# Loading the pieces of the first eight modulation parts two raw chunks sooner on SyncE's queue

## The chip, the cores and the metric

The kernel runs on one core of a Trainium2 chip. The metric is the device time of one execution in microseconds (us), and smaller is better. Three runs of the kernel before gave 2529.38 us in the median (2528.78 to 2529.84). One further execution was recorded by the hardware profiler.

The engines are named as in the profile: PE multiplies matrices, DVE does elementwise work on vectors, ACT applies activations and copies, POOL does little here, and SP only issues transfers (DMAs). Each engine runs its own list of instructions in order, and engines wait for one another through semaphores. All transfers that matter here are issued by SP and go through one queue, which 16 DMA engines serve.

## The reference

Two transformer-like blocks are computed for one sequence of 256 tokens with 2048 features, in float32. The first block begins so:

```python
c_act = jax.nn.silu(c)
mod = c_act @ w_ada[l] + b_ada[l]                 # [2048] x [2048, 12288]
sh1, sc1, gt1, sh2, sc2, gt2 = jnp.split(mod, 6)
h = modulate(rmsnorm(x, g_norm_mix[l]), sh1, sc1)  # h * (1 + sc1) + sh1
proj = h @ w_in[l]                                 # [256, 2048] x [2048, 3072]
```

After it come a recurrent mixer and a pooling mixer, an output product, and a gated feed-forward product; the second block (attention and retention) has no modulation. Only the stretch that the lines above describe is touched by the change. The product with `w_ada` is a vector times a matrix of 100 MB, so it is mostly a matter of bringing the matrix in. The product with `w_in` is real work for PE, but needs `h`, and `h` needs the first two sixths of `mod`, the shift `sh1` and the scale `sc1`.

## The kernel before

**Raw chunks.** Every weight matrix of the big products comes in as chunks of 512 KB (`raw`, 128 partitions x 1024 values). There are 8 buffers for raw chunks. ACT rounds a chunk to its high part (line 1020), DVE subtracts to get the low part (line 1390), and both parts lie in one of 4 buffers (`split`). PE multiplies high and low parts separately (lines 650 and 657 in the wide form, lines 630 to 632 in the narrow form). A chunk is numbered G; PE works through the chunks in order. At step G of their loops, ACT and DVE first finish the sum of chunk G (ACT copies the low half of it from PSUM in the wide form, line 1027; DVE adds it up and so clears the PSUM bank, lines 1410 and 1398) and then convert chunk G + 4. PSUM has two banks for these sums, so PE may begin chunk G once DVE has evacuated chunk G - 2.

**The first product, by quarters.** The 2048 rows of `w_in` are cut into four units of 512. Chunks 0 to 11 hold unit 0 for the 12 column slabs, chunks 12 to 23 unit 1, and chunks 24 to 47 units 2 and 3. So PE can begin with unit 0 of `h` as soon as unit 0 of the modulation is there.

**Pieces and rides.** The columns of `w_ada` for scale and shift of the four units are eight narrow parts (n = 0 to 7: scale and shift of unit 0, then of unit 1, and so on). Each narrow part is loaded in 4 pieces of 1024 KB (`ride`), so there are 32 narrow pieces. They share 4 slots; a piece may be loaded once PE has multiplied the piece four before it (semaphore `ada_multiplied`, line 487 stands behind that wait). The first 8 pieces are multiplied before chunk 0. The other 24 ride in pairs: the list `RIDE_AT` says behind which chunk PE multiplies a pair (line 675): behind chunks 2, 4, 6, 8, 9, 11, 13, 15, 16, 18, 20 and 21. Below, pieces have the numbers 0 to 31, and "the pair of chunk 9" is the one that rides behind chunk 9 (pieces 16 and 17).

**What DVE does with them.** When the four pieces of a part are multiplied, DVE turns the row to columns. For a scale part (`scale_unit`, lines 1441, 1443, 1572, 1529) it also scales the four blocks of `x`; for a shift part (`shift_unit`, lines 1441, 1443, 1534) it makes the low part of `h` after ACT made the high part (line 1074). These steps stand in DVE's loop over G behind the conversion of chunk G + 4: scale of units 1, 2 and 3 at steps 5, 12 and 19, shift of units 1, 2 and 3 at steps 9, 16 and 22. At step 14 stands a short chain on constants of the recurrence (lines 1586 to 1603).

**SP's order.** SP's queue is one list in program order. `LOAD_AT` says before which raw chunk each riding piece is loaded:

```python
        for G in range(2, DOWN_0 + CHUNKS * OUT_SLABS):
            for r, at in enumerate(LOAD_AT):
                if at == G:
                    ...
                        sp.wait_ge(ada_multiplied, free)
                    load_ada(slot, *piece_of(piece))
            ...
            load(G // (2 * CHUNKS), G % (2 * CHUNKS), src)
```

`load` (line 476) waits until the chunk 8 before has been converted. Since SP works in order, a raw chunk that stands behind a pair of pieces is issued only after the waits of that pair.

Pieces after the 31st are wide and belong to later parts (loaded before chunks 30, 36, 38 and so on); still later rows of `w_ada` are added up by DVE.

Of the kernel before, what the change touches and what calls it, by code (L numbers as in the profile page):

```python
# [86 lines left out]
FIRST_WIDE = NARROW * NARROW_PIECES  # L87
# [31 lines left out]
FIRST_RIDE = EARLY * NARROW_PIECES  # L119


def _rides():

    at = [at for at in (2, 4, 6, 8, 9, 11, 13, 15, 16, 18, 20, 21) for _ in range(2)]
    return at + [at for at, _, _ in LATE]


RIDE_AT = _rides()
LOAD_AT = [at + 4 for at in RIDE_AT[:FIRST_WIDE - FIRST_RIDE]]
LOAD_AT += [load for _, _, load in LATE]  # L130
assert len(LATE) == TENSOR_PIECES - FIRST_WIDE
LAST_RIDE = {n: RIDE_AT[min(last_piece(n) - FIRST_RIDE, len(RIDE_AT) - 1)] for n in range(EARLY, TENSOR_PARTS + 1)}
# [51 lines left out]
def build(nc, dram, out):  # L184
# [284 lines left out]
    def _(sp):  # L469
# [26 lines left out]
# [3 lines that stand above are left out]
# [1760 lines left out]
```

## Time and profile before

| | |
|---|---|
| median of 3 runs | 2529.38 us (2528.78 to 2529.84) |
| the profiled execution | 2529.0 us, of which the span of the trace is 2527.1 us |
| PE busy | 2491.0 us (99%) |
| DVE busy | 1834.6 us (73%) |
| ACT busy | 1190.1 us (47%) |
| DMA, all queues | 554.69 MB, 219 GB/s over the span, 391 to 410 GB/s in its first two fortieths |

Busy time is the time in which an engine executes something; the span runs from the first to the last instruction of the trace. The 1.9 us between the span and the time of the profiled execution lie around the trace. In the timelines a row has its start in us from the start of the span, its duration in us, the engine, the line of the kernel, the operation with what it writes and reads, and in square brackets the time that the engine was idle before it with what ended that idle time. Rows of several like instructions are merged, with their count behind an x.

### The profile page before, as it was taken

To read this page: it belongs to the slowest core of one execution; us is meant where nothing else is said; L and a number is where in the kernel's file an instruction comes from. 1 tells how busy PE (TensorE), PEld (TensorE's weight loads), DVE (VectorE), ACT (ScalarE), POOL (GpSimd) and SP (SyncE) were. 2 spreads that over 40 slices of the span, in tenths; PEclk is the share of its full clock that TensorE was granted. 3 is DMA by queue.
4 is the path that set the end of the run, shared out by engine and by line. 5 is a ranking of instruction groups with operands and counts; after the bars stand their busy time and mean duration, and the time that the engine had idled before them with its cause. 6 is when DMAs were issued, how large, how long until landed. Compare 5 with 4: busy or idle time off the path is not lost.

```text
span 2527.1 us, 42169 instructions
## 1 busy us (share of the span) xinstructions
PE 2491.0 (99%) x15708; PEld 2168.1 (86%) x15708; DVE 1834.6 (73%) x2381; ACT 1190.1 (47%) x1458; POOL 18.6 (1%) x54
## 2 busy tenths in 40 slices
PE   7999999999999999999999999999999999999998
PEld 6888888888888888888888888888888888888887
DVE  5678988996556655787785665676888668875886
ACT  3365445544444444654454554455544444444444
POOL 0000000000000000000000000000000000000000
PEclk9999999999999999999999999999999999999999
DMA  9999978797666665566555556556555655566554
GB/s 391 410 391 370 361 265 273 245 342 229 186 189 189 191 202 170 179 204 196 181 165 172 166 184 191 184 192 191 175 199 184 191 187 178 190 200 183 185 173 125
DMA packets 165238, 554.69 MB, mean 219 GB/s; under 512 B 16624, under 2 KB 20720, under 8 KB 165120
## 3 DMA queue, kind: packets, MB, share of 16 engines
q1 hardware_dynamic: 163728, 549.85, 65.0%
q0 software_dynamic: 1392, 3.22, 0.4%
q8 instruction: 80, 1.31, 0.2%
q14 instruction: 38, 0.31, 0.0%
HBM read 550.38 MB, written 2.10 MB: 219 GB/s over the span
## 4 chain that ended last, share of the span: by engine, by line
PE 89%; DVE 6%; DMA 2%; issue 2%; ACT 1%; SPq 0%; DVEq 0%; ACTq 0%
PE ps L650 52%; PE ps L657 26%; PE ps L647 2%; DMA ride<-in_w_ada 2%; PE pm L675 2%; DVE split L1390 2%; DVE acc_ada L1456 1%; PE ps L630 1%; PE ps L654 1%; PE ps L631 1%; PE ps L632 1%; ACT split L1020 0%; DVE val L1408 0%; PE pm L806 0%; DVE x_t L1556 0%
## 5 line engine op out<-in xcount | busy, mean ns | idle before, releaser
L1390 DVE TENSOR_TENSOR split<-raw,split 128x1024 fp32r<-128x1024 f32 (+1 forms) x864 | 1030.8, 1204 | 583.3 <-ACT split L1020 578.6
L1020 ACT ACTIVATE split<-raw 128x1024 fp32r<-128x1024 f32 (+1 forms) x864 | 895.7, 1042 | 1054.3 <-PE ps L657 938.1
L650 PE MATMUL ps<-h_s,split 128*128 128x512 f32 x3592 | 1134.4, 397 | 4.5 <-DVE h_s L1534 2.5
L657 PEld LDWEIGHTS ps<-h_s,split 128*128 128x128 f32 x3592 | 675.9, 188 | 159.9
L650 PE MATMUL ps<-mid_s,split 128*128 128x512 f32 x2336 | 735.0, 396 | 1.0 <-DVE split L1390 0.8
L657 PE MATMUL ps<-h_s,split 128*128 128x256 f32 x3592 | 706.7, 278 | 0.0
L650 PEld LDWEIGHTS ps<-h_s,split 128*128 128x128 f32 x3592 | 548.6, 189 | 9.3 <-issue 5.6
L657 PEld LDWEIGHTS ps<-mid_s,split 128*128 128x128 f32 x2336 | 438.8, 188 | 103.8
L657 PE MATMUL ps<-mid_s,split 128*128 128x256 f32 x2336 | 458.9, 278 | 0.0
L650 PEld LDWEIGHTS ps<-mid_s,split 128*128 128x128 f32 x2336 | 355.6, 189 | 5.0 <-issue 2.7
L1027 ACT ACTIVATE low<-ps 128x512 f32<-128x512 f32 x238 | 138.2, 581 | 22.4 <-PE ps L657 22.4
L1864 DVE SCALAR_TENSOR_TENSOR conv_o<-up_pad,par,conv_o 128x256 f32<-128x256 f32 x176 | 77.5, 482 | 11.4 <-DVE conv_o L1862 5.6
L630 PE MATMUL ps<-h_s,split 128*128 128x256 f32 x288 | 83.6, 290 | 0.0
L631 PE MATMUL ps<-h_s,split 128*128 128x256 f32 x288 | 81.4, 283 | 0.0
L632 PE MATMUL ps<-h_s,split 128*128 128x256 f32 x288 | 81.4, 283 | 0.0
L647 PE MATMUL ps<-split,h_s 128*128 128x512 f32 x256 | 80.8, 397 | 0.0
L675 PE MATMUL pm<-ride,c_act 128*1 128x128 f32 (+1 forms) x1248 | 47.9, 302 | 18.2 <-DMA ride<-in_w_ada 18.2
L1456 DVE SCALAR_TENSOR_TENSOR acc_ada<-add_ffn,c_act,acc_ada 128x1024 f32<-128x1024 f32 x51 | 65.2, 1279 | 0.0
L1410 DVE TENSOR_TENSOR val<-ps,low 128x512 f32<-128x512 f32 x92 | 62.9, 684 | 2.6 <-ACT low L1027 2.6
L1412 DVE TENSOR_TENSOR low<-ps,low 128x512 f32<-128x512 f32 x88 | 60.2, 685 | 3.8 <-ACT low L1027 3.6
L630 PEld LDWEIGHTS ps<-h_s,split 128*128 128x128 f32 x288 | 55.1, 191 | 4.8 <-issue 4.4
L654 PEld LDWEIGHTS ps<-split,h_s 128*128 128x128 f32 x256 | 48.1, 188 | 11.4
(285 smaller groups left out, 1485.4 us busy)
## 6 DMA issues: line engine op xcount, KB each, us to landing
raw<-in_w_in SPq DMA_DIRECT2D x224, 512.0 KB, 3.6
raw<-in_w_ffn_down SPq DMA_DIRECT2D x128, 512.0 KB, 4.2
ride<-in_w_ada SPq DMA_DIRECT2D x46, 1024.0 KB, 11.7
raw<-in_w_ffn_gate SPq DMA_DIRECT2D x88, 512.0 KB, 3.8
raw<-in_w_ffn_up SPq DMA_DIRECT2D x88, 512.0 KB, 4.2
raw<-in_w_ffn_a SPq DMA_DIRECT2D x88, 512.0 KB, 4.1
raw<-in_w_ffn_b SPq DMA_DIRECT2D x88, 512.0 KB, 4.4
raw<-in_w_out SPq DMA_DIRECT2D x64, 512.0 KB, 4.3
```

Of the source, the lines that this page charges most:

```text
L630: pe.matmul(ps[:, s, b, 0:T], weights[:, 0, :], x[:, 0, :], start=start, stop=False)
L631: pe.matmul(ps[:, s, b, 0:T], weights[:, 0, :], x[:, 1, :], start=False, stop=False)
L632: mm = pe.matmul(ps[:, s, b, 0:T], weights[:, 1, :], x[:, 0, :], start=False, stop=stop)
L647: pe.matmul(ps[:, s, b, :], acts[:, k0 + k, 0, b * P:(b + 1) * P], split[:, slot, k, :, :].rearrange("p h n -> p (h n)"), start=start, sto ...
L650: pe.matmul(ps[:, s, b, :], split[:, slot, k, 0, b * P:(b + 1) * P], acts[:, k0 + k, :, :].rearrange("p h t -> p (h t)"), start=start, sto ...
L657: mm = pe.matmul(ps[:, s, b, 0:T], split[:, slot, k, 1, b * P:(b + 1) * P], acts[:, k0 + k, 0, :], start=False, stop=stop)
L675: mm = pe.matmul(pm[2 + n % 2][32 * g:32 * g + 1, 0:32 * blocks].rearrange("p (j q) -> p j q", j=blocks), weights, wide[:, g, :, :], start ...
L1020: act.activation(split[:, c, 0:kt, 0, :], raw[:, CHUNKS * s + c, 0:kt, :], ACT.Copy).then_inc(hi_ready, 1)
L1027: act.activation(low[:, s, :, :], ps[:, s, :, T:2 * T], ACT.Copy).then_inc(low_copied, 1)
L1390: dve.tensor_tensor(split[:, c, 0:kt, 1, :], raw[:, CHUNKS * s + c, 0:kt, :], split[:, c, 0:kt, 0, :].bitcast(F32), ALU.subtract).then_inc ...
L1456: dve.scalar_tensor_tensor(out=sums, in0=piece, scalar=c_act[:, k:k + 1], in1=sums, op0=ALU.mult, op1=ALU.add).then_inc(ada_added, 1)
L1864: ins = dve.scalar_tensor_tensor(out=dst, in0=src, scalar=w, in1=dst, op0=ALU.mult, op1=ALU.add)
```

## The change

The number added to a ride's chunk in `LOAD_AT` falls from 4 to 2 for the 24 narrow riding pieces (8 to 31):

```diff
-LOAD_AT = [at + 4 for at in RIDE_AT[:FIRST_WIDE - FIRST_RIDE]]
+LOAD_AT = [at + 2 for at in RIDE_AT[:FIRST_WIDE - FIRST_RIDE]]
 LOAD_AT += [load for _, _, load in LATE]
```

So the twelve pairs are loaded before raw chunks 4, 6, 8, 10, 11, 13, 15, 17, 18, 20, 22 and 23, where before they stood ahead of chunks 6, 8, 10, 12, 13, 15, 17, 19, 20, 22, 24 and 25. The wide pieces stay where they are. The lists of PE, DVE, ACT and POOL are the same in both kernels; only SP's list differs.

The first place is the start of SP's list, from raw chunk 0 on. `ride` and `ride_89` are two halves of the four slots, and a row stands for like transfers in a row. Before:

```order
L476 DMA raw<-in_w_in 128x1024
L487 DMA ride_89<-in_w_ada 128x4x512 x2
L476 DMA raw<-in_w_in 128x1024 x5
L487 DMA ride<-in_w_ada 128x4x512 x2
L476 DMA raw<-in_w_in 128x1024 x2
L487 DMA ride_89<-in_w_ada 128x4x512 x2
L476 DMA raw<-in_w_in 128x1024 x2
```

And now, at the same place:

```order
L476 DMA raw<-in_w_in 128x1024
L487 DMA ride_89<-in_w_ada 128x4x512 x2
L476 DMA raw<-in_w_in 128x1024 x3
L487 DMA ride<-in_w_ada 128x4x512 x2
L476 DMA raw<-in_w_in 128x1024 x2
L487 DMA ride_89<-in_w_ada 128x4x512 x2
L476 DMA raw<-in_w_in 128x1024 x2
```

The first raw row is chunk 0, and the first pair is pieces 6 and 7. Between pieces 7 and 8 the list had raw chunks 1 to 5, and has chunks 1 to 3 now. Chunks 4 and 5 have moved behind the pair of chunk 2. From there on the pattern of rows repeats with chunk numbers that are two lower: each pair stands two chunks sooner, and each chunk that it passes stands one pair later. Chunks 11 and 18 (and 23 at the end) are passed by two pairs, because the pairs of chunks 8 and 9, of 15 and 16, and of 20 and 21 ride close together.

The second place is the end of the moved stretch on SP, from the pair of chunk 18 to the first wide pair (128x2x1024). Before:

```order
L487 DMA ride_89<-in_w_ada 128x4x512 x2
L476 DMA raw<-in_w_in 128x1024 x2
L487 DMA ride<-in_w_ada 128x4x512 x2
L476 DMA raw<-in_w_in 128x1024
L487 DMA ride_89<-in_w_ada 128x4x512 x2
L476 DMA raw<-in_w_in 128x1024 x5
L487 DMA ride<-in_w_ada 128x2x1024 x2
```

And now:

```order
L487 DMA ride_89<-in_w_ada 128x4x512 x2
L476 DMA raw<-in_w_in 128x1024 x2
L487 DMA ride<-in_w_ada 128x4x512 x2
L476 DMA raw<-in_w_in 128x1024
L487 DMA ride_89<-in_w_ada 128x4x512 x2
L476 DMA raw<-in_w_in 128x1024 x7
L487 DMA ride<-in_w_ada 128x2x1024 x2
```

Behind the last narrow pair (the pair of chunk 21) now follow chunks 23 to 29, where before followed chunks 25 to 29. Chunk 23 stood ahead of the pairs of chunks 20 and 21 and now stands behind both.

## Rows read from the trace of the kernel before

**Rows 1.** The page: PE's busy time over the span, and SP's DMA queue.

```profile
PE 2491.0 (99%) x15708; PEld 2168.1 (86%) x15708; DVE 1834.6 (73%) x2381; ACT 1190.1 (47%) x1458; POOL 18.6 (1%) x54
...
q1 hardware_dynamic: 163728, 549.85, 65.0%
```

**Rows 2.** Stretches in us: length, busy PE, PEld, DVE, ACT, POOL, clock, DMA share, GB/s.

```profile
35.00:140.00 105.00, 101.04 (x1313) 90.56 (x1314) 67.63 (x115) 45.13 (x60) 4.47 (x7) 1.00 1.04 405
44.00:52.00 8.00, 8.00 (x115) 6.84 (x117) 3.91 (x5) 3.54 (x5) 0.00 (x0) 1.00 1.04 411
...
180.00:200.00 20.00, 20.00 (x204) 16.77 (x206) 14.76 (x23) 15.76 (x27) 0.00 (x0) 1.00 0.85 336
```

**Rows 3.** PE's waits from 33 to 140 us: total, times, longest.

```profile
PE pm L675 <- DMA ride<-in_w_ada: 3.6, 3, 2.3
PE ps L650 <- DVE h_s L1534: 0.8, 1, 0.8
```

**Rows 4.** PE's waits from 140 us to the end, the longest in total.

```profile
PE pm L760 <- DVE diag L1503: 2.1, 2, 1.1
PE ps L650 <- DVE h_s L1534: 1.7, 1, 1.7
```

**Rows 5.** PE's timeline: starts of chunks 8, 12, 17, 19, 22; two late rides.

```profile
63.93 0.63 PE L650 MATMUL ps<-h_s,split 128*128 128x512 f32 x2
...
81.66 0.39 PE L630 MATMUL ps<-h_s,split 128*128 128x256 f32 x1
...
103.66 1.05 PE L675 MATMUL pm<-ride,c_act 128*1 128x128 f32 x32 [2.28 <-DMA ride<-in_w_ada]
104.65 0.39 PE L630 MATMUL ps<-h_s,split 128*128 128x256 f32 x1
...
112.44 0.39 PE L630 MATMUL ps<-h_s,split 128*128 128x256 f32 x1
...
125.37 1.05 PE L675 MATMUL pm<-ride,c_act 128*1 128x128 f32 x32 [1.00 <-DMA ride<-in_w_ada]
126.36 0.39 PE L630 MATMUL ps<-h_s,split 128*128 128x256 f32 x1
```

**Rows 6.** ACT's timeline: conversions of chunks 8, 13, 17, 18, 19, 20, 23.

```profile
52.67 1.06 ACT L1020 ACTIVATE split<-raw 128x1024 fp32r<-128x1024 f32 x1 [0.41 <-DMA raw<-in_w_in]
...
74.28 1.06 ACT L1020 ACTIVATE split<-raw 128x1024 fp32r<-128x1024 f32 x1 [1.92 <-DMA raw<-in_w_in]
...
89.53 1.06 ACT L1020 ACTIVATE split<-raw 128x1024 fp32r<-128x1024 f32 x1 [3.58 <-DMA raw<-in_w_in]
92.69 1.06 ACT L1020 ACTIVATE split<-raw 128x1024 fp32r<-128x1024 f32 x1 [2.10 <-PE ps L632]
...
97.21 1.06 ACT L1020 ACTIVATE split<-raw 128x1024 fp32r<-128x1024 f32 x1 [1.81 <-DMA raw<-in_w_in]
104.87 1.06 ACT L1020 ACTIVATE split<-raw 128x1024 fp32r<-128x1024 f32 x1 [6.60 <-DMA raw<-in_w_in]
...
115.69 1.06 ACT L1020 ACTIVATE split<-raw 128x1024 fp32r<-128x1024 f32 x1 [1.95 <-PE ps L632]
```

**Rows 7.** DVE's timeline: conversion of chunk 9; evacuations of chunks 6, 10, 15, 17, 20.

```profile
58.15 1.23 DVE L1390 TENSOR_TENSOR split<-raw,split 128x1024 fp32r<-128x1024 f32 x1 [0.33 <-ACT split L1020]
...
61.62 0.69 DVE L1410 TENSOR_TENSOR pool_x<-ps,low 128x512 f32<-128x512 f32 x1
...
79.35 0.69 DVE L1410 TENSOR_TENSOR gate_p<-ps,low 128x512 f32<-128x512 f32 x1
...
98.78 0.69 DVE L1398 TENSOR_TENSOR xr_pad<-ps,xr_pad 128x512 f32<-128x512 f32 x1
...
109.94 0.68 DVE L1398 TENSOR_TENSOR pool_x<-ps,pool_x 128x512 f32<-128x512 f32 x1
...
120.31 0.69 DVE L1398 TENSOR_TENSOR val<-ps,val 128x512 f32<-128x512 f32 x1
```

**Rows 8.** SP's timeline: issue of the pairs of chunks 16 and 21.

```profile
88.71 1.81 SPq L487 DMA_DIRECT2D ride<-in_w_ada  x2
...
111.70 2.26 SPq L487 DMA_DIRECT2D ride<-in_w_ada  x2
```

**Rows 9.** Pieces by line 487, issue to landing: first 300 us, then first 130 us.

```profile
DMA to landing us min/median/max: 4.8/11.7/18.9
...
DMA to landing us min/median/max: 7.9/12.5/18.9
```

## The prediction

> **What bounds the kernel now.** I read the page first: PE is busy for 2491.0 us of the span, 99%, and SP's queue takes 65.0% of the DMA engines' time over the whole run [rows 1]. So PE bounds the kernel as a whole, and a change of SP's order can matter only where PE waits. Next came the stretches. From 35 to 140 us PE is busy for 101.04 of 105 us, while the DMA share is 1.04 at 405 GB/s; from 180 us on the share falls to 0.85 [rows 2]. So in the stretch that the change touches the queue is full all the time, and PE nearly so. Then PE's waits: from 33 to 140 us it waits 3 times for a piece, 3.6 us in all, the longest 2.3 us [rows 3]. Afterwards it waits for no transfer; its largest groups are 2.1 and 1.7 us on DVE [rows 4]. So what PE has lost or won when chunk 22 begins stays until the end, and I work out just that: PE's start of chunk 22, 126.36 us before [rows 5].
>
> **What the queue does.** With the queue full, the moment at which a transfer lands depends on the bytes ahead of it alone. At 411 GB/s [rows 2] a pair of pieces (2 x 1.049 MB) takes 5.10 us and a raw chunk (0.524 MB) 1.28 us. Two raw chunks and a pair make 7.66 us. The trace has the same period: chunk 19 ends ACT's wait at 97.21 and chunk 20, one pair and one chunk later, at 104.87 [rows 6]; this is 7.66 where 6.38 is due, so 1.28 us of it is a single lateness, which I keep as a separate term. The change deletes and adds no transfer. It lets each pair land sooner by the one or two raw chunks that it passes, 1.28 to 2.56 us, and each passed chunk later by 5.10 us, or 10.2 us for chunks 11, 18 and 23.
>
> The Trainium skill (SBUF — State Buffer, Summary: rules for kernel authors) says to reckon about 358 GB/s for the time of transfers between HBM and SBUF. By that a pair would take 5.86 us and each chunk would be 0.76 us later than I say. The trace moved 411 GB/s [rows 2], so the measurement decides.
>
> **What is removed.** The three late rides, 3.6 us [rows 3]; 2.28 and 1.00 us of them are the second pieces of the pairs of chunks 16 and 21 [rows 5]. Their pieces land 2.5 us and 2.6 us sooner, so I count all of it as gone.
>
> **What is late next: the raw chunks.** They look well covered, since ACT and DVE convert four chunks ahead. But the cover is shorter than it looks. PE may begin chunk G when DVE has evacuated chunk G - 2, and in DVE's list that evacuation stands behind the conversion of chunk G + 1. So chunk G + 1 must have landed, been converted by ACT and DVE, and chunk G - 2 evacuated, before PE begins G. Where a scale or shift step stands between the two, that is added. I take each path from its own rows and shift its landing.
>
> - Chunk 8. Raw chunk 8 landed at 52.67 [rows 6] and now at 57.77. Then ACT 1.06, DVE 1.23, an evacuation 0.69, and from the conversion of chunk 9 (with the scale step of unit 1) to the end of the evacuation of chunk 6 62.31 - 58.15 = 4.16 us [rows 7]. The sum is 64.9 to 65.0 us, where PE began at 63.93 [rows 5]: +1.0.
> - Chunk 12. Raw chunk 13 landed at 74.28 and the evacuation of chunk 10 ended at 79.35 + 0.69 = 80.04, with the shift step of unit 1 between: 5.76 us [rows 6, 7]. Now 74.28 + 5.10 + 5.76 = 85.14, where PE began at 81.66 [rows 5]: +3.5.
> - Chunk 17. PE carries +3.5 into it and wins back the wait of 2.28 us: +1.2 without a new wait. Raw chunk 18 now stands behind the pair of chunk 16, whose second piece landed at 103.62 (0.04 before its ride [rows 5]); without chunk 19 ahead it is 102.3 us, or 101.1 if the single lateness of 1.28 us falls behind it. ACT began this chunk at 92.69 and the evacuation of chunk 15 ended at 99.47, with the chain of constants between: 6.78 us [rows 6, 7]. So PE begins at 109.2 (or 107.9) against 104.65 [rows 5]: +4.5 (or +3.3).
> - Chunk 19. At PE's own pace the same shift. Raw chunk 20: 104.87 + 5.10 + (110.62 - 104.87) = 115.7 against 112.44 [rows 5 to 7]: +3.3, not above what PE carries.
> - Chunk 22. PE wins back 1.00 us: +3.5 (or +2.3). Raw chunk 23 now lands where the last piece landed, less chunk 24: 125.33 - 1.28 = 124.05. From ACT's start at 115.69 to the end of the evacuation of chunk 20 at 121.00 it took 5.31 us [rows 6, 7]. So PE begins at 129.4 at the soonest, against 126.36 [rows 5]: +3.0.
>
> **Does the queue run dry?** Every pair waits until the pair two before it has been multiplied, and now more of SP's list stands behind that wait. The pair of chunk 16 was issued at 88.71 [rows 8] on the ride behind chunk 13, which is 3.5 us later now: 92.2. To follow raw chunk 17 (89.53 + 5.10 = 94.6 [rows 6]) without a gap, its first piece must land at 97.2, 5.0 us after issue. The pair of chunk 21 was issued at 111.70 [rows 8] on the ride behind chunk 18: with +4.5 this is 116.2, and it should land at 120.2, 4.0 us after issue. What a piece takes that meets an empty queue no row shows just so. From below, the shortest landing in the first 300 us is 4.8 us; from above, the shortest in the loaded stretch is 7.9 us [rows 9]. I take 4.8, since the 7.9 us of the loaded stretch are mostly waiting behind other bytes. By 4.8 the first has no gap and the second one of 0.8 us, which puts chunk 22 at 130.2: +3.9. With +3.3 at chunk 17 there is no gap, and chunk 22 stands at +3.0. Between these I take +3.5.
>
> The Trainium skill (DMA: Bandwidth & Descriptors, Anatomy of one DMA) gives about 2.0 us plus bytes over 436 GB/s for a DMA on the GpSimd path, which would be an estimate of 4.4 us for a piece; the gap would be 0.4 us, and the end +3.5. No run here shows a lone piece that fast, so the bound from the row stays.
>
> Nothing else changes: the other engines' lists are the same, and the pieces' slots are given free by the same rides. Chunk 25 and all behind it have the same bytes ahead of them as before, and PE comes to them 3 us later, so they have more cover than before.
>
> **The sum.** Old waits go, -3.6; new waits come, +7.1 (1.0 at chunk 8, 2.8 at chunk 12, 2.1 to 3.3 at chunk 17, what is left by chunk 22), so that chunk 22 begins 3.5 us later. The profiled execution took 2529.0 us (span 2527.1 and 1.9 around it), 0.4 under the median of the runs. The forecast is 2529.4 + 3.5 = 2532.9 us, +0.14%. A change below 0.2%, some 5.1 us, is about what a measurement of this kernel cannot tell from none, so I call this the same, on the slow side.
>
> **Rivals.**
> A. The raw chunks have enough cover, and only the late rides go. For it: ACT's conversions start four chunks ahead, and two of those I use began on PE's signal with the chunk long landed (92.69 and 115.69 [rows 6]). Against it: five of the seven rows there end on the DMA. The time would be 2529.4 - 3.6 = 2525.8 us.
> B. The loop of rides, slots and loads feeds on itself, so that the kernel is slower by more than the bound. Its place is SP's wait for a slot: once a pair is issued later than the queue needs it, every chunk behind is late by the gap, PE rides later still, and the next pair is issued later. It decides from the point at which a pair meets an empty queue. With 7.9 us a piece in place of 4.8, the pair of chunk 16 leaves a gap of 2.9 us, and that of chunk 21 at least 1.6 us more: 3.5 + 4.5 = +8.0, 2537.4 us. For it: margins of 0.2 and -0.8 us above. Against it: the queue's backlog in that stretch is why 7.9 was seen.
> C. The order changes little, because the pairs are issued on the rides anyway, at the same instants. Then the pieces land hardly sooner, and the chunks find the queue emptier than I reckon: within 1 us of before, 2529.4 us. Against it: the queue is full at 1.04 [rows 2], so each byte that is moved ahead delays what is behind it.
>
> **How the numbers follow.** The forecast (+1.5 to +5) has 0.61, A (-3.6 to -1) 0.12, B (above +5.1) 0.19, C 0.08. A can pass -0.2% only if PE gained more than the 3.6 us that it waits, so faster gets 0.02; slower is B and a little of the forecast's edge, 0.20; the same has the rest, 0.78. The range leaves out most of A below and the upper part of B above: 2528.5 to 2536.5 us.
>
> **What would show it.** Right: PE's wait for pieces after 33 us falls to almost nothing, and PE waits for evacuations by DVE instead, at chunk 8 (about 1 us), chunk 12 (2.8), chunk 17 (2 to 3) and, smaller, near chunk 22; ACT waits longer for raw chunks; PE begins chunk 12 near 85.1 and chunk 22 near 129.9; behind it PE has no new wait. Wrong: if PE begins chunk 12 before 83, raw chunks are not 5.10 us later, or the path from landing to PE is shorter; if the DMA share falls below 1 between 90 and 125 us by more than a slice, the queue ran dry and B holds; if the shift at chunk 22 does not stay until the end, something behind absorbs it.

## The result and the profile after

The changed kernel takes 2537.24 us in the median of 7 runs (2534.98 to 2539.99), the kernel before 2529.21 us (2527.98 to 2529.84) beside it. The ratio is 1.0034, with a 95% interval of 1.0025 to 1.0043: slower by some 8.0 us. The forecast was 2532.9 us with a range up to 2536.5, so the time lies outside. One of the twelve executions of the kernel e5 below took 4947.2 us and counts in neither its median nor its ratio.

The page of the changed kernel, in the two lines that answer to [rows 1]:

```profile
PE 2491.9 (98%) x15708; PEld 2170.5 (86%) x15708; DVE 1833.2 (72%) x2381; ACT 1190.2 (47%) x1458; POOL 18.6 (1%) x54
...
q1 hardware_dynamic: 163728, 549.85, 64.7%
```

Over the span PE is busy for 0.9 us more than before and idle for 7.4 us more. That does not say that it loses by waiting alone, since a chunk at a lower clock counts as busy. Its waits from 33 to 145 us, as in [rows 3]:

```profile
PE ps L630 <- DVE xr_pad L1398: 3.3, 1, 3.3
PE ps L630 <- DVE gate_p L1410: 2.7, 1, 2.7
PE ps L630 <- DVE val L1398: 2.0, 1, 2.0
PE ps L650 <- DVE pool_x L1410: 1.0, 1, 1.0
```

The waits for pieces are gone, 3.6 us of them, and four waits for evacuations by DVE stand in their place, 9.0 us. PE's timeline shows where they are; these are the starts of chunks 8, 12, 17, 18, 19, 22 and 23, where [rows 5] had the starts around them:

```profile
65.05 0.50 PE L650 MATMUL ps<-h_s,split 128*128 128x512 f32 x1 [0.96 <-DVE pool_x L1410]
...
85.31 0.39 PE L630 MATMUL ps<-h_s,split 128*128 128x256 f32 x1 [2.68 <-DVE gate_p L1410]
...
109.23 0.58 PE L630 MATMUL ps<-h_s,split 128*128 128x256 f32 x1 [3.31 <-DVE xr_pad L1398]
...
114.52 0.41 PE L630 MATMUL ps<-h_s,split 128*128 128x256 f32 x1
...
119.46 0.39 PE L630 MATMUL ps<-h_s,split 128*128 128x256 f32 x1
...
134.23 0.39 PE L630 MATMUL ps<-h_s,split 128*128 128x256 f32 x1 [1.96 <-DVE val L1398]
...
138.68 0.29 PE L630 MATMUL ps<-h_s,split 128*128 128x256 f32 x1
```

Chunks 8, 12 and 17 begin at 65.05, 85.31 and 109.23, where the forecast had 65.0, 85.1 and 109.2. Up to here it holds to 0.2 us. Then it fails: the row at 114.52 is the start of chunk 18, so chunk 17 took 5.29 us, against 2.97 from chunk 17 to 18 in the trace of before. The row at 138.68 is the start of chunk 23; chunk 22 took 4.45 us. The stretches tell why. Columns as in [rows 2], the clock and the DMA share at the end of a row:

```profile
93.00:101.00 8.00, 8.00 (x121) 7.45 (x113) 3.13 (x5) 1.06 (x1) 0.00 (x0) 1.00 0.99 346
109.20:114.50 5.30, 5.27 (x24) 5.27 (x25) 3.44 (x5) 1.47 (x2) 0.00 (x0) 0.50 1.04 412
115.00:119.00 4.00, 4.00 (x75) 3.80 (x77) 3.82 (x7) 1.75 (x3) 0.00 (x0) 1.00 0.67 263
134.00:138.70 4.70, 4.47 (x25) 4.48 (x26) 3.22 (x4) 0.00 (x0) 1.53 (x3) 0.64 1.04 343
```

During chunk 17 the granted clock of TensorE is 0.50, that is 1.2 of 2.4 GHz, right behind PE's wait of 3.31 us; during chunk 22 it is 0.64 in the mean, behind a wait of 1.96 us. (The clock falls in the wait itself: from 106.0 to 109.0 us, while PE does nothing, it is 0.83.) And the DMA share, 1.04 before from 35 to 140 us [rows 2], falls to 0.99 and 0.67 in two stretches, and the rate from 405 to 346 and 263 GB/s: the queue ran short. SP's issues of the pairs of chunks 16 and 21, as in [rows 8]:

```profile
92.38 1.88 SPq L487 DMA_DIRECT2D ride<-in_w_ada  x2
...
118.72 1.24 SPq L487 DMA_DIRECT2D ride<-in_w_ada  x2
```

The first pieces of the two took 5.9 and 5.0 us to land (the view of DMA issues, in windows that hold one piece each; the last column is the time from issue to landing):

```profile
ride<-in_w_ada SPq DMA_DIRECT2D x1, 1024.0 KB, 5.9
...
ride<-in_w_ada SPq DMA_DIRECT2D x1, 1024.0 KB, 5.0
```

ACT's conversions of chunks 17, 18, 20, 22 and 23, as in [rows 6], all end on the DMA now:

```profile
94.75 1.06 ACT L1020 ACTIVATE split<-raw 128x1024 fp32r<-128x1024 f32 x1 [5.13 <-DMA raw<-in_w_in]
102.42 1.06 ACT L1020 ACTIVATE split<-raw 128x1024 fp32r<-128x1024 f32 x1 [6.60 <-DMA raw<-in_w_in]
...
111.25 1.06 ACT L1020 ACTIVATE split<-raw 128x1024 fp32r<-128x1024 f32 x1 [5.18 <-DMA raw<-in_w_in]
...
119.33 1.06 ACT L1020 ACTIVATE split<-raw 128x1024 fp32r<-128x1024 f32 x1 [2.58 <-DMA raw<-in_w_in]
128.86 1.06 ACT L1020 ACTIVATE split<-raw 128x1024 fp32r<-128x1024 f32 x1 [8.47 <-DMA raw<-in_w_in]
```

The first piece of the pair of chunk 16 could have landed at 94.7 + 2.55 = 97.3, right behind raw chunk 17; it landed at 92.38 + 5.9 = 98.3, so the gap is 1.0 us. That of the pair of chunk 21 could have landed at 119.3 + 2.55 = 121.9 and came at 118.72 + 5.0 = 123.7: a gap of 1.8 us. The raw chunks behind came later still. A pair and a chunk take 6.38 us in a full queue; from chunk 17 to 18 it took 102.42 - 94.75 = 7.67 us, and from chunk 22 to 23 128.86 - 119.33 = 9.53 us, so chunk 18 lost 1.3 us and chunk 23 3.15 us. Why chunk 23 lost more than the gap ahead of its pair is not shown. After chunk 23 PE has no new wait above 0.2 us.

The starts of PE's chunks in the kernels that follow, as differences in us to the trace of before (one profiled execution each; chunk 0 itself varies by up to 0.6 us):

| kernel | 8 | 12 | 17 | 18 | 19 | 22 | 23 |
|---|---|---|---|---|---|---|---|
| changed kernel | +1.1 | +3.65 | +4.6 | +6.9 | +7.0 | +7.9 | +9.35 |
| e1, idle products at 12, 17, 22 | +1.4 | +3.9 | +4.95 | +4.95 | +5.4 | +5.8 | +5.7 |
| e2, idle products at 17 | +1.7 | +4.2 | +6.5 | +6.5 | +6.5 | +7.2 | +8.7 |
| e3, first six pairs sooner | +1.3 | +3.7 | +1.3 | +1.3 | +1.3 | +0.1 | +0.1 |
| e4, last six pairs sooner | +0.1 | +0.1 | +3.35 | +4.9 | +4.9 | +5.8 | +5.8 |
| e6, constants first | +1.3 | +3.7 | +1.25 | +1.3 | +4.8 | +5.3 | +5.3 |
| e7, three chunks behind | +0.5 | +0.1 | -0.9 | -0.7 | -0.6 | -1.2 | -0.9 |
| e8, three pairs alone | +0.2 | +0.2 | -1.2 | -0.9 | +0.05 | -1.0 | -0.7 |

e5 has two pairs of rides elsewhere, so of it the chunks with the same work ahead are told below.

### The profile page after: what moved, and what is told of

Its sections match the earlier page's. It is cut to its first block, busy times and chain, and to the rows that moved or that the text cites. A ratio compares the mean times of both kernels' runs of the same rounds, so it can differ in the third digit from the quotient of the medians.

```text
span 2535.4 us, 42169 instructions
## 1 busy us (share of the span) xinstructions
PE 2491.9 (98%) x15708; PEld 2170.5 (86%) x15708; DVE 1833.2 (72%) x2381; ACT 1190.2 (47%) x1458; POOL 18.6 (1%) x54
## 4 chain that ended last, share of the span: by engine, by line
PE 87%; DVE 7%; DMA 3%; issue 2%; ACT 1%; SPq 0%; DVEq 0%; ACTq 0%
PE ps L650 52%; PE ps L657 25%; PE ps L647 2%; DMA raw<-in_w_in 2%; DVE split L1390 2%; DVE acc_ada L1456 1%; PE ps L630 1%; PE ps L631 1%; PE ps L632 1%; PE ps L654 1%; PE pm L675 1%; DMA ride<-in_w_ada 1%; ACT split L1020 1%; DVE val L1408 0%; PE pm L806 0%
```

## The experiments

The theory after the result: the late bytes do what the forecast says; what came on top is that PE's clock falls to half at a wait, and that the queue has gaps where SP waits for a slot. The rival is B of the prediction: the loop of rides, slots and loads grows by itself.

**e1 and e2: PE kept busy.** Products that nothing reads are multiplied ahead of PE's waits, in the changed kernel; e2 has `{17: 12}` alone.

```diff
         def quarter_slab(G):
+            keep_busy({12: 8, 17: 12, 22: 7}.get(G, 0))
             if G >= 2:
                 pe.wait_ge(evacuated, G - 1)
```

Expected of e1:

> The changed kernel, with idle products (128x128, nothing reads them) on PE ahead of its waits at chunks 12 (8 of them, 2.0 us), 17 (12, 3.0 us) and 22 (7, 1.8 us), so that PE works through the waits. Theory (PE's clock falls to half after a wait, and the products at half clock are what came on top of the waits): the granted clock stays 1.00 from 109 to 139 us, chunk 17 takes 2.97 us where it took 5.3, chunk 22 begins 4 to 5 us later than before and not 7.9, and the time is 2533 to 2534 us, near what was forecast. Rival (the loop of rides, slots and loads feeds on itself, the clock does not matter): 2536.5 to 2538, as the changed kernel.

Measured: 2534.22 us, ratio 1.0022 (1.0012 to 1.0031). The same stretches of e1:

```profile
109.20:114.50 5.30, 4.90 (x41) 4.90 (x42) 3.50 (x5) 1.06 (x1) 0.00 (x0) 1.00 1.03 406
115.00:119.00 4.00, 3.65 (x80) 3.15 (x79) 3.48 (x7) 2.51 (x5) 0.00 (x0) 1.00 0.94 332
134.00:138.70 4.70, 4.70 (x42) 4.70 (x41) 3.41 (x5) 1.58 (x3) 0.00 (x0) 1.00 1.04 301
```

The clock is 1.00 in all three, chunk 17 takes 2.97 us again, and the DMA share from 115 to 119 us is 0.94 where it was 0.67. The loss against the kernel before (2528.79 us beside it) is 5.4 us where it was 8.0, so holding the clock up is worth 2.6 us of the median; but the time is above the expected 2534 by 0.2 us, and chunk 22 begins 5.8 us late where 4 to 5 was expected. Something besides the clock was still missing. ACT's conversions of chunks 17, 18, 22 and 23 in e1:

```profile
95.01 1.06 ACT L1021 ACTIVATE split<-raw 128x1024 fp32r<-128x1024 f32 x1 [5.14 <-DMA raw<-in_w_in]
102.77 1.06 ACT L1021 ACTIVATE split<-raw 128x1024 fp32r<-128x1024 f32 x1 [6.71 <-DMA raw<-in_w_in]
...
119.53 1.06 ACT L1021 ACTIVATE split<-raw 128x1024 fp32r<-128x1024 f32 x1 [2.02 <-DMA raw<-in_w_in]
126.66 1.06 ACT L1021 ACTIVATE split<-raw 128x1024 fp32r<-128x1024 f32 x1 [6.07 <-DMA raw<-in_w_in]
```

From chunk 17 to 18 it is 7.76 us and from chunk 22 to 23 7.13 us, so 1.4 and 0.75 us are still lost in the queue at full clock; the second gap has shrunk with the slow chunk.

Expected of e2:

> The changed kernel, with 12 idle products ahead of the wait at chunk 17 alone. Theory (clock): chunk 17 takes 2.97 us, so 2.3 us go there, and the gap in the queue at the pair of chunk 21 shrinks by up to 1.8 us; the wait at chunk 22 may still bring the clock down (1.5 us). 2533.5 to 2535.5 us. Rival (loop): 2536.5 to 2538.

Measured: 2535.69 us, ratio 1.0029 (1.0019 to 1.0038), a little above the range of the theory and below that of the rival. In its profile chunk 17 has its full clock, but half clock came behind the wait at chunk 12 instead. PE's row at that chunk, and the stretches of chunks 12 and 22:

```profile
85.84 0.39 PE L630 MATMUL ps<-h_s,split 128*128 128x256 f32 x1 [2.68 <-DVE gate_p L1411]
```

```profile
85.80:90.30 4.50, 4.46 (x24) 4.46 (x25) 3.05 (x3) 1.75 (x3) 0.00 (x0) 0.62 1.03 406
...
133.50:138.00 4.50, 4.43 (x24) 4.43 (x25) 3.07 (x4) 0.00 (x0) 1.49 (x3) 0.62 1.04 352
```

The wait at chunk 12 is 2.68 us in this execution and in that of the changed kernel. There the clock stayed at 1.00 and chunk 12 took 2.98 us; here it took 4.5. In the profiles of e3 and e6 waits of 2.69 and 2.68 us at this chunk left the clock at full again. So the length of a wait alone does not decide.

**e3 and e4: half of the pairs.** The edit of e3; in e4 the 2 and the 4 change places.

```diff
-LOAD_AT = [at + 2 for at in RIDE_AT[:FIRST_WIDE - FIRST_RIDE]]
+LOAD_AT = [at + (2 if at <= 11 else 4) for at in RIDE_AT[:FIRST_WIDE - FIRST_RIDE]]
```

Expected of e3:

> Only the six pairs of chunks 2 to 11 are loaded two chunks sooner, those of chunks 13 to 21 stand as before. Theory (each place is one path from a landing to PE, and a later place with cover takes the shift back): chunk 8 +1.1, chunk 12 +3.65 as in the changed kernel, but chunk 17 only +1.2 to +1.5 and chunk 22 +0.2 to +0.6; 2529.4 to 2530.0 us. Rival (loop: a late ride makes the next load late, so a shift stays or grows): +3.7 or more at chunk 22, 2533 and above.

Measured: 2529.05 us, ratio 1.0001 (0.9992 to 1.0010), 0.35 us below the expected range, with chunk 22 at +0.1 where +0.2 to +0.6 was expected. PE's starts of chunks 12, 17 and 22:

```profile
85.38 0.39 PE L630 MATMUL ps<-h_s,split 128*128 128x256 f32 x1 [2.69 <-DVE gate_p L1410]
...
105.91 0.39 PE L630 MATMUL ps<-h_s,split 128*128 128x256 f32 x1
...
126.44 0.39 PE L630 MATMUL ps<-h_s,split 128*128 128x256 f32 x1
```

The wait at chunk 12 is the same as in the changed kernel, and by chunk 22 all of it has been given back, since the late rides of before (2.28 and 1.00 us [rows 5]) simply become shorter waits. So a shift of 3.7 us does not feed on itself as such. B's own place, a pair that meets an empty queue, e3 does not reach: the later pairs stand as before, and the queue stays full.

Expected of e4:

> Only the six pairs of chunks 13 to 21 are loaded two chunks sooner, those of chunks 2 to 11 stand as before. Theory (the paths of chunks 17 and 22 and the clock set the end): nothing until chunk 12, +4.6 at chunk 17 with a wait of over 4 us, chunk 17 at half clock (+2.3), a gap in the queue at the pair of chunk 21; 2535.5 to 2538 us, like the changed kernel. Rival (the shifts of the first half add to those of the second): about half of the loss, 2533.

Measured: 2535.26 us, ratio 1.0026 (1.0016 to 1.0036), 0.2 us below the expected range and far from the rival's 2533. PE waits 3.69 us at chunk 17 and 2.08 us at chunk 22; the stretch of chunk 17 and one behind it:

```profile
108.00:112.50 4.50, 4.50 (x25) 4.50 (x26) 3.01 (x4) 1.06 (x1) 0.00 (x0) 0.62 1.03 406
114.50:118.00 3.50, 3.50 (x78) 3.07 (x77) 3.21 (x5) 1.37 (x3) 0.00 (x0) 1.00 0.43 135
```

Half clock and a gap again, without any shift from the first half. Chunk 17 itself begins 1.25 us sooner than expected, and PE also waits 1.06 us at chunk 15, which was not expected. Most of the loss, 6.5 of 8.0 us, belongs to the last six pairs.

**e5: the gaps taken away.** As e1 (8, 8 and 4 idle products), and the rides of two pairs stand one chunk sooner on PE, so that SP issues the pairs of chunks 16 and 21 2.8 and 4.1 us sooner than in e1. The order of the transfers, and the step of the scale part on DVE, stay.

```diff
+RIDE_AT = [{13: 12, 18: 17}.get(at, at) if r < FIRST_WIDE - FIRST_RIDE else at for r, at in enumerate(RIDE_AT)]
...
+LAST_RIDE[6] = 18
```

> As the kernel with idle products at chunks 12, 17 and 22 (8, 8 and 4 of them here), and the rides of the pairs of chunks 13 and 18 stand one chunk sooner on PE (behind chunks 12 and 17), so that the slots of the pairs of chunks 16 and 21 come free 3 us sooner; the order of the transfers and DVE's steps stay. Theory (beside the clock, the rest over the forecast is gaps in the queue at these two pairs, where SP waits for a slot): the pair of chunk 16 lands right behind raw chunk 17 and the pair of chunk 21 right behind raw chunk 22, chunk 17 begins +3.7 to +4.5 after before and chunk 22 +3.5 to +4.5, where the kernel with idle products alone has +4.95 and +5.76; 2532 to 2533.2 us against its 2534.2. Rival (the rest is late bytes from elsewhere, the gaps are hidden): as that kernel, +5.7 at chunk 22 and 2534 to 2534.5.

Measured: 2532.11 us, ratio 1.0012 (1.0003 to 1.0021). Three stretches, PE's starts of chunks 17 and 22, and ACT's conversions of chunks 17, 18, 22 and 23 (lines are two or three higher in this kernel):

```profile
93.00:101.00 8.00, 8.00 (x114) 7.79 (x117) 3.49 (x6) 1.06 (x1) 0.00 (x0) 1.00 1.03 406
...
100.00:104.00 4.00, 4.00 (x74) 3.73 (x63) 1.30 (x2) 2.35 (x3) 0.00 (x0) 1.00 0.88 296
...
115.00:119.00 4.00, 4.00 (x35) 4.00 (x34) 2.92 (x5) 1.15 (x2) 0.00 (x0) 1.00 1.04 412
```

```profile
108.33 0.39 PE L632 MATMUL ps<-h_s,split 128*128 128x256 f32 x1
...
130.46 0.39 PE L632 MATMUL ps<-h_s,split 128*128 128x256 f32 x1 [0.43 <-DVE val L1401]
```

```profile
95.11 1.06 ACT L1023 ACTIVATE split<-raw 128x1024 fp32r<-128x1024 f32 x1 [5.17 <-DMA raw<-in_w_in]
101.50 1.06 ACT L1023 ACTIVATE split<-raw 128x1024 fp32r<-128x1024 f32 x1 [5.33 <-DMA raw<-in_w_in]
...
118.69 1.06 ACT L1023 ACTIVATE split<-raw 128x1024 fp32r<-128x1024 f32 x1 [2.85 <-DMA raw<-in_w_in]
125.09 1.06 ACT L1023 ACTIVATE split<-raw 128x1024 fp32r<-128x1024 f32 x1 [5.33 <-DMA raw<-in_w_in]
```

The two gaps are gone: from chunk 17 to 18 it is 6.39 us and from chunk 22 to 23 6.40 us, where 6.38 is due. Chunk 17 begins +3.7 and chunk 22 +4.1 after before, as expected, and the loss is 3.1 us (2532.11 against 2528.97), 2.3 us less than that of e1. The fewer idle products are not the reason: in e1 PE still waits 0.7 and 0.6 us behind them at chunks 12 and 17, and chunk 22 begins at 132.12, right behind the evacuation of chunk 20, which ends at 131.99. But the 3.1 us are not the price of the late bytes alone. From 100 to 104 us the queue runs short here too, at the pair of chunk 18, whose first piece takes 6.0 us to land; the changed kernel and e1 have the same dip (350 and 364 GB/s in that stretch), and no run takes it away. The working of the prediction had +3.0 for chunk 22 without a gap.

**e6: another path shortened.** In the changed kernel the chain of constants at step 14 moves ahead of the conversion of chunk 18, on ACT and DVE.

```diff
-            ahead(G)
             if G == LAMBDA_AT:
                 lru_constants()
+            ahead(G)
```

> The changed kernel, with the chain of constants at step 14 ahead of the conversion of chunk 18 on ACT and DVE, where DVE only waits for that chunk. Theory (each place is a path from a landing to PE): chunk 17 loses its wait of 3.3 us and begins near +1.3, but the next path, raw chunk 20 through the shift step of unit 2, is as late as before, so the wait appears at chunk 19 (about 3 us, +4.5); the gap at the pair of chunk 21 shrinks, since the ride behind chunk 18 is sooner; 2533 to 2535.5 us. Rival (the chain of constants is what the change costs): 2529.5 to 2531 us.

Measured: 2534.62 us, ratio 1.0022 (1.0013 to 1.0031). PE's start of chunk 19, and the stretch of that chunk:

```profile
117.25 0.39 PE L630 MATMUL ps<-h_s,split 128*128 128x256 f32 x1 [3.47 <-DVE pool_x L1398]
```

```profile
117.20:121.70 4.50, 4.45 (x24) 4.46 (x25) 2.45 (x3) 1.06 (x1) 0.00 (x0) 0.62 1.04 408
```

The wait at chunk 17 is gone, and the next path gives one of 3.47 us at chunk 19, with low clock behind it. The loss is 5.65 us, 2.4 us less than that of the changed kernel and far from the rival's 0.5 to 2: taking out one path helps little while the chunks of the next are as late. In this profile the pair of chunk 21 is issued at 112.96 and leaves no gap.

**e7 and e8: less of the change.** In e7 the number added to a ride's chunk in `LOAD_AT` is 3 for all pairs; in e8 it is 3 for those of chunks 9, 16 and 21 alone and 4, as before, for the others. The line of e7, and that of e8:

```diff
+LOAD_AT = [at + 3 for at in RIDE_AT[:FIRST_WIDE - FIRST_RIDE]]
...
+LOAD_AT = [at + (3 if at in (9, 16, 21) else 4) for at in RIDE_AT[:FIRST_WIDE - FIRST_RIDE]]
```

> The pairs are loaded three chunks behind their ride's number, halfway between the two kernels: each pair passes one raw chunk and each passed chunk is 5.1 us later. Theory (paths): waits of about 0.4 us at chunk 8 and 0.8 to 1.3 us at chunk 15 (raw chunk 16 through the scale step of unit 2), the late ride at chunk 16 shrinks from 2.3 to about 1 us and the others vanish; chunk 22 begins -0.5 to -1.3, 2527.5 to 2528.5 us. Rival (any passed chunk costs PE its lateness, or the loop runs): half of the loss or more, 2533.

> Only the pairs of chunks 9, 16 and 21, the ones that ride close behind another pair and came late, are loaded one raw chunk sooner. Theory: their waits shrink by 1.28 us each (to 0, 1.0 and 0), and chunks 12, 19 and 24, 5.1 us later, have cover, save perhaps chunk 24: chunk 22 begins -2 to -2.6, chunk 23 -0.9 or sooner; 2527.5 to 2528.3 us. Rival: no change that can be measured in either direction, 2528.8.

Measured: e7 2527.92 us, ratio 0.9997 (0.9988 to 1.0005), and e8 2528.15 us, ratio 0.9996 (0.9988 to 1.0005). Neither can be told from no change, though both medians are lower. In the profile of e7 PE waits 0.3 us at chunk 8 and 1.22 us at chunk 15, and begins chunk 22 1.2 us sooner than before:

```profile
93.88 0.39 PE L630 MATMUL ps<-h_s,split 128*128 128x256 f32 x1 [1.22 <-DVE xr_pad L1398]
...
125.13 0.39 PE L630 MATMUL ps<-h_s,split 128*128 128x256 f32 x1
```

Both waits are of the expected size; the late rides wait 0.4 us where about 1 was expected. In e8 chunk 22 begins 1.0 us sooner where 2 to 2.6 was expected; the late rides still wait 1.9 us in all, where 1.0 was expected. No kernel here beats the one before beyond its interval.

## Why the prediction was wrong

**Where the time went.** By medians, each against the kernel before beside it: 3.1 us are left in e5 (the late bytes, and the dip at the pair of chunk 18), 2.3 us are the gaps at the pairs of chunks 16 and 21 (e1 over e5), 2.6 us the clock with what it adds to the second gap (changed kernel over e1); together the 8.0 us measured. The split between neighbours is rougher than these digits: the intervals of e1 and e5, and of e1 and the changed kernel, overlap, and what tells the three apart are the clock, the DMA share and ACT's rows. In the profile the +9.35 us at chunk 23 are 5.4 us more of waits and 3.8 us of two slow chunks.

- *What bounds the kernel, and that the start of chunk 22 is what stays.* Right in kind: e1's +5.7 at chunk 23 stands at +5.4 in the time. But the stretch to follow ended one chunk later, since chunk 22 itself ran slow. And some 1 us did not stay: DVE's sum at 320.38 us before comes 9.34 us later in the changed kernel, that at 346.90 us 8.30 us later. Between them every profile here has a stretch of low clock; the mean clock from 320 to 360 us is 0.87 before and 0.91 in the changed kernel.
- *What is removed.* Right: no ride waits for a piece behind 33 us.
- *What is late next.* Right, path by path: chunks 8, 12 and 17 to 0.2 us; e3, e5 and e6 each moved as these paths say. At chunk 17 the size is in part luck: the forecast had raw chunk 18 at 102.3 by the lateness of 1.28 us and without a gap. It came at 102.42, but by a gap; in e5, without the gap, it came at 101.50, near the other figure of the prediction, 101.1, with the lateness behind it.
- *Does the queue run dry?* The term was mis-sized. It was priced at 4.8 us for a lone piece, which gave no gap at the pair of chunk 16 and 0.8 us at that of chunk 21. Measured were 5.9 and 5.0 us, with 2.4 and 0.6 us of other bytes still to land ahead of them, and gaps of 1.0 and 1.8 us (1.3 and 3.15 us for the raw chunks behind). The second grew because the ride behind chunk 18 came later: the pair was issued at 118.72, not 116.2. The pair of chunk 18 was not reckoned at all: it was issued at 100.18, its first piece took 7.2 us, and the queue dipped there too.
- *"Nothing else changes."* This is the step that failed. The new waits were counted as waiting only. Behind two of them PE multiplied at half clock: chunk 17 took 2.3 us and chunk 22 1.5 us more. The sum had no term for it, and neither had the range: its upper end would have had to hold the +3.9 of the forecast and some 4 us for the clock. The trace of before shows both cases. Its wait of 2.28 us at 103.66 [rows 5] was followed by a chunk of 2.97 us. But at the waits of [rows 4], which the prediction passed over, the clock did fall:

```profile
330.00:335.00 5.00, 2.60 (x8) 2.14 (x9) 3.53 (x11) 2.77 (x6) 0.00 (x0) 0.50 0.13 54
...
333.62 1.19 PE L650 MATMUL ps<-h_s,split 128*128 128x512 f32 x2 [1.72 <-DVE h_s L1534]
```

Two such matmuls take 0.63 us at 63.93 [rows 5] and 1.19 us here, behind several waits of at most 1.72 us. The Trainium skill (TensorE: Matmul & The Clock Gate, Part 1) has the 1.2 GHz as the clock of an idle TensorE; the granted 0.50 of the changed kernel agrees with that level. I had not weighed it.
- *Rival B.* Its number, 2537.4 us, was met, but by its mechanism only in part, so the agreement is luck. Its gaps were to be 2.9 and 1.6 us; they were 1.0 and 1.8. A late ride does make a late issue and a gap, as B says, at full clock too (e1 over e5, 2.3 us). What B does not have is the clock: a slow chunk makes the next ride later still, and the second gap grows from 0.75 us in e1 to 3.15 us in the changed kernel, both for raw chunk 23.
- *Rivals A and C.* Both fell: the raw chunks had too little cover, and each came later by what was moved ahead of it.

## What to carry to other kernels

When a queue is full, moving a transfer ahead makes everything that it passes later by its bytes, and a buffer of many chunks does not show how much cover there is: follow one chunk from its landing through every in-order step that stands before the engine's next start. A wait that a change puts into a dense row of matmuls costs more than its length when the clock falls at it (1.5 to 2.3 us more here), so give every new wait of PE of the size of those above a second price in the range, the next chunk at half clock, and look in the trace of before for stretches where the clock already falls. And where a queue's issue waits for a slot, compare the time from that release to the moment when the queue empties with what a transfer takes that meets a short queue (5.0 to 7.2 us here), not with the shortest one seen.

## What the runs showed of the hardware that was not expected

- TensorE at a granted clock of 0.50 behind a wait of 3.31 us, for the whole of a chunk (109.2 to 114.5 us), in a kernel that is busy 98% of its span. In the mean of some 4.5 us it was 0.62 to 0.64 behind waits of 1.86 (e2, chunk 22), 1.96 (the changed kernel, chunk 22), 2.68 (e2, chunk 12), 3.47 (e6) and 3.69 us (e4), and 1.00 behind waits of 2.08 (e4, chunk 22), 2.28 (the kernel before) and again 2.68 us (the changed kernel, chunk 12). In the kernel before it is 0.50 from 330 to 335 us, where no wait is longer than 1.72 us but PE is busy for 2.60 of 5 us. What decides between them stays open here.
- One and the same stretch of low clock differs by execution. From 320 to 360 us the mean clock is 0.87 in six of the ten profiles (before, e1, e5, e6, e7, e8) and 0.91 in four (the changed kernel, e2, e3, e4); in these four the shift against before falls by 1.0 to 1.2 us between 320 and 347 us, in the others by at most 0.3 us.
- The changed kernel spreads over 5.0 us in 7 runs, the kernel before over 1.9 us in its 7. That the clock makes this spread is only argued.
- A piece of 1024 KB that met a short queue took 5.0 us with 0.6 us of other bytes still to land and 5.9 us with 2.4 us of them; the shortest before, in the first 300 us, was 4.8 us.
